# Expert steps of 1,792 hidden units in a one-core diffusion backbone with routed experts

## The chip, the cores and the metric

The kernel runs on 1 core of one Trainium2 chip. The metric is device time in microseconds (us) of one execution; three runs of the kernel before took 1365.89, 1367.7 and 1370.32 us (median 1367.7). The profile is of one more execution, 1364.95 us long.

## The reference, cut to what matters

Two layers over 256 latent tokens of width 1024. Layer 0 is attention and a dense SwiGLU; layer 1 is a pooling mixer and then the part that the change is about, 8 experts of 3,584 hidden units of which each token takes two:

```python
def swiglu(h, w_gu, w_down):
    g, u = jnp.split(h @ w_gu, 2, axis=-1)
    return (jax.nn.silu(g) * u) @ w_down

def moe_swiglu(h, router_w, router_b, w_gu, w_down):
    logits = (h @ router_w).astype(jnp.float32) + router_b.astype(jnp.float32)
    top_v, top_i = lax.top_k(logits, TOP_K)
    gates = jax.nn.softmax(top_v, axis=-1)
    combine = jnp.einsum('btk,btke->bte', gates, jax.nn.one_hot(top_i, N_EXPERTS, dtype=jnp.float32))
    y = jnp.zeros(h.shape, jnp.float32)
    for e in range(N_EXPERTS):
        y = y + combine[..., e:e + 1] * swiglu(h, w_gu[e], w_down[e]).astype(jnp.float32)
    return y.astype(h.dtype)
```

All is float32. The weights of the experts are 8 x 3 x 1024 x 3584 x 4 bytes, 352.3 MB, and each byte is read once.

## The kernel before, in words

The program is written out by hand, engine by engine, with semaphores; nothing schedules it. After the router, the tokens of each expert are gathered into units of 32 slots (`x_all`). In this data the eight experts have 2, 5, 2, 2, 2, 4, 2 and 1 units, 20 in all.

**Steps.** The hidden units of an expert are cut into 4 pieces of 896 (`MS`). A step is one piece of one expert; a round is one step for each of the 8 experts, and there are 4 rounds, so 32 steps. A step has three phases on PE: the gate pass for every unit of the expert, then the up pass for every unit, then the down pass for every unit. The partial results of the 4 rounds are summed in `y_all`.

**Weights and their ring.** A step needs three chunks of 3.67 MB: gate, up, down. They lie in a ring of 5 slots (`RING`, `w_gu`, `w_dn`), chunk c in slot c mod 5. SP issues the loads in the order of use (`load`, `after_step`); ahead of each it waits on the semaphore which says that the chunk five places earlier is used up: a chunk of gate or up is free after the last unit's pass, by halves where the semaphore `pass_half` or `down_half` allows it. A chunk of gate or up comes in 4 DMAs of 896 KB with rows of 896 x 4 = 3,584 bytes (two rows for each partition and DMA); a chunk of down comes in two, with contiguous runs of 16,384 and 12,288 bytes. The first 5 chunks are loaded while the layer before is still at work.

**A pass.** `gate_or_up` runs 8 blocks of the contraction times 4 column tiles of 224 (`W`), in two halves of 4 blocks which go to two PSUM banks. Each half increments `pass_half` or `pass_done`. ACT takes the first half out of PSUM (`take_half`), DVE adds the second (`take_rest`); for gate, ACT then applies SiLU into `kept`; for up, DVE multiplies, transposes and writes the activation back to `kept` (`activate`). POOL brings the tokens (`bring_slots`) and the activations (`bring_act`) of the next unit into place. `down` runs 7 blocks times 4 tiles of 256, again in two halves (4 and 3 blocks), and DVE adds both into `y_all` (`add_rows`). DVE goes in order: it first finishes the `activate` of the last unit, and only then takes the first unit's down result.

**Loops.** PE's program is a loop over 5 steps (the ring's period); inside, each phase is a loop over the units, whose number comes from a register.

**End.** After the last round the rows of `y_all` go to DRAM (`put_rows`), are fetched back by token (`picked`), normalised, and added to the tokens `tok`, which have stayed in SBUF since the mixer.

Of the kernel before, what the change touches and what calls it, by code (L numbers as in the profile page):

```python
# [27 lines left out]
P = 128  # L28
# [21 lines left out]
MS = 896  # L50
MSTEPS = FE // MS
MQ = MS // P
UNIT = 32
# [10 lines left out]
KINDS = 3  # L64
RING = 5
CHUNK = KC * MS * 4
# [67 lines left out]
def build(nc, x, c, ctx_in, c_ctx, ada_w, ada_b, norm_g, w_qkv, w_o, sink, pool_w, pool_b, pool_scale,  # L134
# [10 lines left out]

    w_gu = [sb(f"w_gu{x}", [P, KC, MS], F32, R0 + CHUNK * x) for x in range(RING)]
    w_dn = [sb(f"w_dn{x}", [P, MQ, D], F32, R0 + CHUNK * x) for x in range(RING)]
# [85 lines left out]
    top_i = sb("top_i", [P, 2 * E], U32, S[5] + 4 * KB + 640)  # L233
    y_rows = nc.dram_tensor("y_rows", (SLOTS, D), F32).ap()
# [13 lines left out]
    def col(a, n):  # L248
        return cols[:, a:a + n]
# [14 lines left out]
    R_D, R_EX, R_DEN, R_G1, R_G2 = 48, 50, 52, 54, 56  # L264
# [29 lines left out]
    def bank(i):  # L294
# [14 lines left out]
        halves_free gated_up act_turned act_kept act_lo act_hi down_half down_done y_half y_added late_ident_in places_ready y_written picked0 picked1 f_ready  # L309
# [45 lines left out]
    def _(sp):  # L355
# [36 lines left out]

        GATE, UP, DOWN = range(KINDS)

        def load(x, kind, e, step, parts=range(4)):

            for part in parts:
                if kind == DOWN:
                    if part % 2:
                        continue  # L400
                    rows = slice(2 * part, min(2 * part + 4, MQ))
                    to = w_dn[x][:, rows, :]
                    src = mdn_v[bass.ds(e, 1), bass.ds(step, 1), :, rows, :].rearrange("e s p q n -> p (e s q) n")
                else:
                    rows = slice(2 * part, 2 * part + 2)
                    to = w_gu[x][:, rows, :]
                    src = mgu_v[bass.ds(e, 1), :, rows, bass.ds(step * MS + kind * FE, MS)].rearrange("e p k n -> p (e k) n")
                sp.dma_start(to, src).then_inc(s[f"w_{x}{part // 2}"], 32 if kind == DOWN else 16)  # L408

        load(0, GATE, 0, 0, (0, 1, 2))  # L410
        sp.wait_ge(s["f_split0"], FSTEPS)
        load(0, GATE, 0, 0, (3,))
        sp.wait_ge(s["f_split1"], FSTEPS)
        load(1, UP, 0, 0, (0,))
        sp.wait_ge(s["f_split2"], FSTEPS)
        load(1, UP, 0, 0, (1,))
        sp.wait_ge(s["acc_ready"], (EARLY + L1_LATE) * KC)
        load(3, GATE, 1, 0, (2, 3))
        sp.wait_ge(s["f_used1"], FSTEPS)
        sp.wait_ge(s["f_used2"], FSTEPS)  # L420
        load(2, DOWN, 0, 0, (2,))
        load(3, GATE, 1, 0, (0, 1))
        sp.wait_ge(s["f_used2"], FSTEPS + 1)
        load(1, UP, 0, 0, (2, 3))
        load(2, DOWN, 0, 0, (0,))
        sp.wait_ge(s["poolmix_ready"], TB)
        load(4, UP, 1, 0, (0, 1))
        sp.wait_ge(s["gathered"], 2 * KC)
        load(4, UP, 1, 0, (2, 3))
# [7 lines left out]
        sp.reg_mov(step, 1)  # L437
# [7 lines left out]
        def after_step(t, last=False):  # L445

            next_count(sp, left, n, digit)
            sp.reg_add(gone, gone, n)
            sp.reg_add(passes, passes, n)
            at = place(step)  # L450
            sp.wait_ge(s["pass_done"], passes)
            load(KINDS * t % RING, DOWN, *at)
# [14 lines left out]
        with sp.Fori(0, (STEPS - 2) // RING):  # L467
            for t in range(RING):
                after_step(t)
        assert (STEPS - 2) % RING == 0  # L470
        after_step(STEPS - 2, last=True)
# [24 lines left out]
    def _(pool):  # L496
# [23 lines left out]
        for b in range(TB):  # L520
# [3 lines left out]
        p, d, row, first, at, n, digit = (pool.alloc_register(name) for name in (  # L524
            "pool_pass", "pool_down", "pool_row", "pool_first", "pool_kept", "pool_n", "pool_digit"))
# [4 lines left out]
        pool.reg_mov(d, 1)  # L530

# [10 lines left out]
        def bring_act():  # L542

            a = kept[:, bass.ds(pool.snap(at, min_val=0, max_val=MOST - 1), 1), :].rearrange("p a (q n) -> p (a q) n", n=UNIT)
            pool.wait_ge(s["act_kept"], d)
# [3 lines left out]
            pool.tensor_copy(act_cur[:, 4:MQ, :], a[:, 4:MQ, :]).then_inc(s["act_hi"], 1)  # L549
# [3 lines left out]
        with pool.Fori(0, MSTEPS):  # L553
            pool.reg_mov(first, 0)
            with pool.Fori(0, E):
# [5 lines left out]
                pool.reg_mov(at, 0)  # L561
                with pool.Fori(0, n):
                    bring_act()
# [30 lines left out]
    def _(pe):  # L594
# [408 lines left out]
        def gate_or_up(x, fills):  # L1003

            for half, (bank_, taken, brought) in enumerate(((HALF_BANK, "half_taken", "x_lo"), (REST_BANK, "rest_taken", "x_hi"))):
                pe.wait_ge(s[brought], p)
                pe.wait_ge(s[taken], p)
                pe.wait_ge(s[f"w_{x}{half}"], fills * 32)
                for k in range(4 * half, 4 * half + 4):
                    for t in range(TILES):  # L1010
                        mm = pe.matmul(ps[UNIT * t:UNIT * t + UNIT, bank_, 0:W], x_cur[:, k, :],  # L1011
                                       w_gu[x][:, k, W * t:W * t + W], start=(k % 4 == 0), stop=(k % 4 == 3))
# [805 lines left out]
```

## Time and profile before

| what | value |
|---|---|
| median of 3 runs | 1367.7 us |
| the profiled execution | 1364.95 us, of which the span is 1363.3 us |
| PE busy | 1207.2 us, 89% of the span |
| chain that ended last | PE 67%, DMA 13%, SPq 9%, issue 4%, DVE 4% |
| weights of the experts, issued by SP | 256 DMAs of 896 KB, 32 of 2048 KB, 32 of 1536 KB |
| bytes moved | 461.09 MB, mean 338 GB/s |
| expert stage | from 492.94 us (first pass) to 1337.4 us (last down pass) |

The span is the time from the first to the last instruction on the chip; the execution's own time is 1.65 us more. PE and DMA busy shares near the top at the same time are read stage by stage: the question is which of the two waits for the other.

### The profile page before, as it was taken

What the parts mean: (1) busy time and instruction counts of PE and PEld (TensorE: products, weight loads), DVE (VectorE), ACT (ScalarE), POOL (GpSimd) and SP (SyncE); (2) the same over time, 40 slices, a digit from 0 to 9 for tenths busy, and PEclk for the clock granted to TensorE, in tenths of its full rate; (3) what the DMA queues carried; (4) which work ended last, traced back from release to release, by engine and by line L of the source; (5) the groups of instructions that cost most, each with busy time, mean ns of one, the idle gap of its engine ahead of it and who ended that gap; (6) DMA issues with size and microseconds to landing.
All of it is one profiled execution on the core that took longest, in us unless ns stands there. A gap on an engine that the chain in (4) does not pass through costs nothing.

```text
span 1363.3 us, 43424 instructions
## 1 busy us (share of the span) xinstructions
PE 1207.2 (89%) x16928; PEld 850.5 (62%) x16928; DVE 578.1 (42%) x1110; ACT 316.2 (23%) x535; POOL 169.1 (12%) x518
## 2 busy tenths in 40 slices
PE   4998998999999699998979899968998986999982
PEld 1456975788888576665646466646765643666751
DVE  0588845787775543232222233312332321323322
ACT  2005644334433422111102012111111100211111
POOL 1010000000010111111111111101111110111111
PEclk8899999999999699998989899988998988999995
DMA  9995121688899348899999999999999999999996
GB/s 338 390 366 189 63 93 31 222 293 292 290 337 406 154 174 347 333 410 412 416 409 411 385 408 410 411 414 413 410 410 415 412 410 413 414 385 411 412 416 205
DMA packets 129070, 461.09 MB, mean 338 GB/s; under 512 B 8240, under 2 KB 34016, under 8 KB 120672
## 3 DMA queue, kind: packets, MB, share of 16 engines
q1 hardware_dynamic: 114368, 403.78, 75.4%
q0 software_dynamic: 13952, 55.58, 11.0%
q8 instruction: 68, 1.11, 0.3%
q10 hardware_dynamic: 672, 0.54, 0.1%
q14 instruction: 10, 0.08, 0.0%
HBM read 455.81 MB, written 4.06 MB: 337 GB/s over the span
## 4 chain that ended last, share of the span: by engine, by line
PE 67%; DMA 13%; SPq 9%; issue 4%; DVE 4%; ACT 1%; POOL 0%; POOLq 0%; DVEq 0%; ACTq 0%
PE ps L1011 28%; PE ps L1025 14%; SPq L408 9%; DMA w_gu<-in_moe_w_gu 6%; PE ps L870 4%; PE ps L694 4%; PE ps L822 2%; PE ps L824 2%; PE ps L823 2%; DMA ctx_tok<-in_ctx 2%; PE ps L812 2%; PE ps L754 2%; DMA w_dn<-in_moe_w_down 2%; DMA ada<-in_ada_w 1%; DMA f_raw<-in_ffn_w_gu 1%
## 5 line engine op out<-in xcount | busy, mean ns | idle before, releaser
L1011 PE MATMUL ps<-w_gu,x_cur 128*32 128x224 f32 x10240 | 513.4, 362 | 60.0 <-issue 29.1
L1011 PEld LDWEIGHTS ps<-w_gu,x_cur 128*32 128x32 f32 x10240 | 356.9, 113 | 213.8 <-issue 74.9
L1025 PE MATMUL ps<-w_dn,consts_sb 128*32 128x256 f32 x4480 | 260.4, 386 | 22.3 <-DMA w_dn<-in_moe_w_down 12.2
L1729 DVE TENSOR_TENSOR cols<-cols,ps 128x224 f32<-128x224 f32 x160 | 91.9, 575 | 414.0 <-PE ps L1011 414.0
L1025 PEld LDWEIGHTS ps<-w_dn,consts_sb 128*32 128x32 f32 x4480 | 151.4, 111 | 124.0 <-issue 34.9
L1271 ACT ACTIVATE cols<-ps 128x224 f32<-128x224 f32 x160 | 93.7, 586 | 559.7 <-PE ps L1011 435.7
L1399 DVE SCALAR_TENSOR_TENSOR ada_acc<-ada,cols,ada_acc 128x512 f32<-128x512 f32 x140 | 105.0, 750 | 4.0
L1530 DVE TENSOR_TENSOR f_lo<-f_raw,f_hi 128x2048 fp32r<-128x2048 f32 x32 | 73.1, 2292 | 46.9 <-ACT f_hi L1159 45.6
L536 POOL COPY x_cur<-x_all 128x128 f32 x160 | 47.0, 294 | 317.5 <-PE ps L1011 270.3
L1159 ACT ACTIVATE f_hi<-f_raw 128x2048 fp32r<-128x2048 f32 x32 | 61.0, 1915 | 64.5 <-DMA f_raw<-in_ffn_w_gu 60.5
L822 PE MATMUL ps<-f_hi,hf_hi 128*128 128x512 f32 x176 | 71.1, 404 | 2.9 <-DVE f_act L1571 2.8
L538 POOL COPY x_cur<-x_all 128x128 f32 x160 | 47.0, 293 | 186.6 <-PE ps L1011 186.6
L824 PE MATMUL ps<-f_hi,hf_lo 128*128 128x512 f32 x176 | 69.2, 393 | 0.0
L823 PE MATMUL ps<-f_lo,hf_hi 128*128 128x512 f32 x176 | 69.1, 393 | 0.0
L1286 ACT ACTIVATE kept<-cols 128x224 f32 x80 | 31.2, 390 | 147.8 <-DVE cols L1729 147.8
L1756 DVE TENSOR_TENSOR y_all<-y_all,ps 128x256 f32 x60 | 25.3, 422 | 81.2 <-PE ps L1025 70.0
L1759 DVE TENSOR_TENSOR y_all<-y_all,ps 128x256 f32 x80 | 33.7, 421 | 57.1 <-PE ps L1025 57.1
L547 POOL COPY consts_sb<-kept 128x128 f32 x80 | 23.5, 293 | 175.5 <-DVE kept L1744 106.8
L694 PE MATMUL ps<-wqkv,hT 128*128 128x512 f32 x96 | 42.5, 596 | 1.1 <-DVE hT L1370 1.1
L822 PEld LDWEIGHTS ps<-f_hi,hf_hi 128*128 128x128 f32 x176 | 33.5, 190 | 11.4 <-issue 3.4
L511 POOL DMA_DIRECT2D ada<-in_ada_w x10 | 8.8, 883 | 250.3 <-DVE ada_acc L1399 250.3
L824 PEld LDWEIGHTS ps<-f_hi,hf_lo 128*128 128x128 f32 x176 | 33.3, 189 | 7.2
(236 smaller groups left out, 1074.7 us busy)
## 6 DMA issues: line engine op xcount, KB each, us to landing
w_gu<-in_moe_w_gu SPq DMA_DIRECT2D x256, 896.0 KB
w_dn<-in_moe_w_down SPq DMA_DIRECT2D x32, 2048.0 KB
w_dn<-in_moe_w_down SPq DMA_DIRECT2D x32, 1536.0 KB
ada<-in_ada_w POOLq DMA_DIRECT2D x23, 2048.0 KB, 10.0
f_raw<-in_ffn_w_gu SPq DMA_DIRECT2D x44, 512.0 KB, 6.7
f_raw<-in_ffn_w_down SPq DMA_DIRECT2D x11, 1024.0 KB, 5.0
wqkv<-in_attn_w_qkv SPq DMA_DIRECT2D x3, 2048.0 KB, 19.5
wo_sb<-in_attn_w_o SPq DMA_DIRECT2D x1, 4096.0 KB, 23.7
```

The source lines that it names most:

```text
L408: sp.dma_start(to, src).then_inc(s[f"w_{x}{part // 2}"], 32 if kind == DOWN else 16)
L694: mm = pe.matmul(bank(3 + u % 4), src[:, k, b * P:(b + 1) * P], wqkv[:, k, 512 * n:512 * n + 512], start=(k == 0), stop=(k == KC - 1))
L822: pe.matmul(bank(1 + b), hi, f_hi[k][:, kk, :], start=first, stop=False)
L823: pe.matmul(bank(1 + b), hi, f_lo[k][:, kk, :], start=False, stop=False)
L824: mm = pe.matmul(bank(1 + b), lo, f_hi[k][:, kk, :], start=False, stop=last)
L1011: mm = pe.matmul(ps[UNIT * t:UNIT * t + UNIT, bank_, 0:W], x_cur[:, k, :], w_gu[x][:, k, W * t:W * t + W], start=(k % 4 == 0), stop=(k % 4 ...
L1025: mm = pe.matmul(ps[UNIT * t:UNIT * t + UNIT, bank_, 0:OW], act_cur[:, q, :], w_dn[x][:, q, OW * t:OW * t + OW], start=(q == rows[0]), sto ...
L1159: act.activation(f_hi[k][:], f_raw[k][:], ACT.Copy).then_inc(s[f"f_hi{k}"], 1)
L1271: act.activation(halves.rearrange("p (q c) -> p c q", q=MQ), ps[:, HALF_BANK, 0:W].rearrange("p (c q) -> p c q", q=MQ), ACT.Copy).then_inc ...
L1399: ins = dve.scalar_tensor_tensor(acc_q[:], w[:, k, :], v, acc_q[:], ALU.mult, ALU.add)
L1530: dve.tensor_tensor(lo[:], f_raw[k][:], hi[:].bitcast(F32), ALU.subtract).then_inc(s[f"f_split{k}"], 1)
L1729: dve.tensor_tensor(view, view, ps[:, REST_BANK, 0:W].rearrange("p (c q) -> p c q", q=MQ), ALU.add).then_inc(s["rest_taken"], 1)
```

## The change

A step is now 1,792 units, so there are 2 rounds and 16 steps. A step has six chunks of the same 3.67 MB: gate, low half of the contraction (rows 0 to 511 of the model width) and high half, up low and high, down rows low and high. A pass of a unit reads two chunks, low then high. The loads of gate and up are still 896 KB each, with one row of 1,792 x 4 = 7,168 bytes for each partition. The down phase runs in two parts, over all units each, with one chunk each. The ring still has 5 slots. To make room for the wider `kept`, the tokens are written to DRAM after the mixer (`tok_away`) and read back at the end (`tok_back`); a few small columns move to `cols`.

```diff
-MS = 896
+MS = 1792
+DQ = MQ // 2
+KH = KC // 2
-KINDS = 3
+KINDS = 6
 RING = 5
-CHUNK = KC * MS * 4
+CHUNK = KH * MS * 4
...
-                    rows = slice(2 * part, 2 * part + 2)
-                    to = w_gu[x][:, rows, :]
+                    up, k = divmod(kind, 2)
+                    to = w_gu[x][:, part:part + 1, :]
...
+        load(4, DOWN_LO, 0, 0, (0,))
+        sp.wait_ge(s["y_normed"], 6)
+        sp.dma_start(tok_away, tok[:].rearrange("p b d -> p (b d)")).then_inc(s["tok_kept"], 16)
...
         def after_step(t, last=False):
+            slot = [(KINDS * t + kind) % RING for kind in range(KINDS)]
...
-            sp.wait_ge(s["pass_done"], passes)
-            load(KINDS * t % RING, DOWN, *at)
+            sp.wait_ge(s["pass_half"], passes)
+            load(slot[GATE_LO], DOWN_HI, *at)
             sp.reg_add(step, step, 1)
...
+            sp.wait_ge(s["pass_done"], passes)
+            load(slot[GATE_HI], GATE_LO, *at)
             sp.reg_add(passes, passes, n)
             sp.wait_ge(s["pass_half"], passes)
-            load((KINDS * t + 1) % RING, GATE, *at, parts=(0, 1))
+            load(slot[UP_LO], GATE_HI, *at)
             sp.wait_ge(s["pass_done"], passes)
-            load((KINDS * t + 1) % RING, GATE, *at, parts=(2, 3))
+            load(slot[UP_HI], UP_LO, *at)
+            sp.reg_add(gone, gone, n)
             sp.wait_ge(s["down_half"], gone)
-            load((KINDS * t + 2) % RING, UP, *at, parts=(0, 1))
+            load(slot[DOWN_LO], UP_HI, *at, parts=(0, 1))
             sp.wait_ge(s["down_done"], gone)
-            load((KINDS * t + 2) % RING, UP, *at, parts=(2, 3))
+            load(slot[DOWN_LO], UP_HI, *at, parts=(2, 3))
+            sp.reg_add(gone, gone, n)
+            sp.wait_ge(s["down_half"], gone)
+            load(slot[DOWN_HI], DOWN_LO, *at, parts=(0,))
+            sp.wait_ge(s["down_done"], gone)
+            load(slot[DOWN_HI], DOWN_LO, *at, parts=(2,))
...
+        sp.wait_ge(s["tok_kept"], 16)
+        sp.dma_start(tok_back[:].rearrange("p b d -> p (b d)"), tok_away).then_inc(s["tok_back_in"], 16)
...
-        def gate_or_up(x, fills):
+        def gate_or_up(low, high):
...
-                pe.wait_ge(s[f"w_{x}{half}"], fills * 32)
-                for k in range(4 * half, 4 * half + 4):
+                for k in range(KH):
+                    if k % 2 == 0:
+                        pe.wait_ge(s[f"w_{x}{k // 2}"], fills * 32)
...
+            with pe.Fori(0, n):
+                gate_or_up(chunks[0], chunks[1])
+            with pe.Fori(0, n):
+                gate_or_up(chunks[2], chunks[3])
+            for part in range(2):
+                with pe.Fori(0, n):
+                    down(*chunks[4 + part])
```

Two places show how the instructions stand. The first is SP's queue in the loop over the steps, at the load that waits for the end of the first gate phase; `w_dn_55` and `w_gu_51` are slots 0 and 1 of the ring. Before:

```order
L408 ISA [waits pass_done]
L408 DMA w_dn_55<-in_moe_w_down 128x4096
L408 ISA
L408 DMA w_dn_55<-in_moe_w_down 128x3072
...
L408 ISA [waits pass_half]
L408 DMA w_gu_51<-in_moe_w_gu 128x2x896
...
L408 ISA [waits pass_done]
L408 DMA w_gu_51<-in_moe_w_gu 128x2x896
...
L408 ISA [waits down_half]
L408 DMA w_gu_52<-in_moe_w_gu 128x2x896
```

After (slots 2, 3 and 4 are `w_gu_52` to `w_gu_54`):

```order
L415 ISA [waits pass_half]
L415 DMA w_dn_55<-in_moe_w_down 128x4096
...
L415 ISA [waits pass_done]
L415 DMA w_gu_51<-in_moe_w_gu 128x1792
...
L415 ISA [waits pass_half]
L415 DMA w_gu_52<-in_moe_w_gu 128x1792
...
L415 ISA [waits pass_done]
L415 DMA w_gu_53<-in_moe_w_gu 128x1792
...
L415 ISA [waits down_half]
L415 DMA w_gu_54<-in_moe_w_gu 128x1792
```

One chunk was released by the gate phase, one by the up phase and one by the down phase; now two chunks wait for the end of the gate phase, the next two for the end of the up phase.

The second is PE's queue in the first step. Before, a pass reads one slot and the down pass follows:

```order
L1011 MATMUL ps<-w_gu_50,x_cur 32x224 [waits w_00]
L1011 MATMUL ps<-w_gu_50,x_cur 32x224 x15
L1011 MATMUL ps<-w_gu_50,x_cur 32x224 [waits w_01,rest_taken,x_hi]
...
L1011 MATMUL ps<-w_gu_51,x_cur 32x224 [waits w_10]
...
L1025 MATMUL ps<-w_dn_57,consts_sb 32x256 [waits w_20]
```

After:

```order
L1038 MATMUL ps<-w_gu_50,x_cur 32x448 [waits w_00]
L1038 MATMUL ps<-w_gu_50,x_cur 32x448 x7
...
L1038 MATMUL ps<-w_gu_51,x_cur 32x448 [waits w_10,rest_taken,x_hi]
...
L1038 MATMUL ps<-w_gu_52,x_cur 32x448 [waits w_20]
...
L1038 MATMUL ps<-w_gu_53,x_cur 32x448 [waits w_30,rest_taken,x_hi]
...
L1052 MATMUL ps<-w_dn_59,act_cur 32x256 [waits w_40]
...
L1052 MATMUL ps<-w_dn_55,act_cur 32x256 [waits w_00]
```

A pass has as many matmuls as before, of twice the columns, and alternates between two slots for each unit, so both are held until the last unit is through.

## Rows read from the trace of the kernel before

**Rows 1.** The page: the span

```profile
span 1363.3 us, 43424 instructions
```

**Rows 2.** Windows of the expert stage: engines busy, granted clock, DMA share, GB/s

```profile
490.00:520.00 30.00, 27.66 (x554) 18.89 (x556) 9.55 (x18) 6.46 (x13) 5.35 (x19) 1.00 0.82 317
520.00:545.00 25.00, 25.00 (x524) 17.28 (x512) 10.90 (x24) 5.38 (x11) 4.77 (x16) 1.00 0.83 323
545.00:580.00 35.00, 34.58 (x683) 22.86 (x684) 10.50 (x24) 3.78 (x8) 6.43 (x23) 1.00 0.84 335
...
780.00:830.00 50.00, 49.37 (x996) 32.31 (x988) 17.20 (x40) 8.84 (x17) 9.04 (x33) 1.00 0.97 389
...
880.00:930.00 50.00, 36.94 (x605) 23.57 (x596) 10.67 (x25) 4.84 (x10) 5.48 (x20) 0.86 1.02 412
...
1180.00:1230.00 50.00, 49.59 (x992) 32.21 (x988) 18.02 (x42) 6.46 (x12) 9.20 (x33) 1.00 0.98 395
```

**Rows 3.** Timeline of PE: start, us, line, records (two for each matmul)

```profile
492.94 12.31 PE L1011 MATMUL ps<-w_gu,x_cur 128*32 128x224 f32 x256 [2.12 <-POOL x_cur L536]
...
511.54 30.45 PE L1011 MATMUL ps<-w_gu,x_cur 128*32 128x224 f32 x640
...
545.23 12.29 PE L1025 MATMUL ps<-w_dn,consts_sb 128*32 128x256 f32 x224 [0.21 <-DVE y_all L1754]
557.33 12.29 PE L1011 MATMUL ps<-w_gu,x_cur 128*32 128x224 f32 x256
...
773.47 15.07 PE L1011 MATMUL ps<-w_gu,x_cur 128*32 128x224 f32 x256 [5.86 <-issue]
```

**Rows 4.** Windows with one kind of weights in flight (columns as in rows 2)

```profile
1227.00:1240.00 13.00, 12.79 (x264) 8.48 (x260) 5.13 (x12) 2.51 (x5) 2.44 (x9) 1.00 1.03 405
1242.00:1248.00 6.00, 6.00 (x136) 4.25 (x128) 0.99 (x2) 1.58 (x3) 0.88 (x3) 1.00 1.02 427
1253.00:1266.00 13.00, 11.50 (x228) 7.45 (x220) 4.16 (x11) 1.15 (x2) 2.18 (x8) 1.00 1.03 405
1268.00:1274.00 6.00, 6.00 (x132) 5.01 (x128) 1.13 (x2) 1.93 (x4) 1.18 (x4) 1.00 1.03 430
```

**Rows 5.** Timeline of SP's queue: start and length of the issues

```profile
499.90 1.05 SPq L408 DMA_DIRECT2D w_dn<-in_moe_w_down  x2
504.02 11.95 SPq L408 DMA_DIRECT2D w_gu<-in_moe_w_gu  x8
```

**Rows 6.** The DMA view of 496 to 504 us, in 40 slices

```profile
DMA  9999761000000000000000309903246899599599
```

**Rows 7.** Waits of PE in 492 to 1340 us: total, times, longest

```profile
PE ps L1011 <- issue: 29.1, 5, 5.9
```

**Rows 8.** DVE's groups by form: busy, mean ns, idle before

```profile
L1729 DVE TENSOR_TENSOR cols<-cols,ps 128x224 f32<-128x224 f32 x160 | 91.9, 575 | 414.0 <-PE ps L1011 414.0
...
L1530 DVE TENSOR_TENSOR f_lo<-f_raw,f_hi 128x2048 fp32r<-128x2048 f32 x32 | 73.1, 2292 | 46.9 <-ACT f_hi L1159 45.6
...
L1742 DVE STREAM_TRANSPOSE actT<-cols 128x224 f32<-128x224 f32 x80 | 32.9, 411 | 2.7
L1740 DVE TENSOR_TENSOR cols<-cols,kept 128x224 f32<-128x224 f32 x80 | 32.2, 402 | 11.9 <-DVE cols L1729 0.2
L1756 DVE TENSOR_TENSOR y_all<-y_all,ps 128x256 f32 x60 | 25.3, 422 | 81.2 <-PE ps L1025 70.0 <-DVE kept L1744 11.2
L1744 DVE TENSOR_SCALAR kept<-actT 128x224 f32 x80 | 24.6, 308 | 2.8
```

**Rows 9.** Timeline of the end of the kernel

```profile
1327.77 0.35 SPq L476 DMA_DIRECT2D late_ident<-in_consts  x1
...
1328.25 10.67 SPq L345 DMA_DIRECT2D y_rows<-y_all  x10
...
1334.63 2.79 PE L1025 MATMUL ps<-w_dn,consts_sb 128*32 128x256 f32 x24 [1.17 <-DMA w_dn<-in_moe_w_down]
...
1342.94 1.01 POOL L569 DMA_INDIRECT picked<-y_rows,rows_i  x1 [12.60 <-DMA y_rows<-y_all]
```

More of the change, by code:

```diff
@@ L391, in _ @@
             dense_step(st)
-        GATE, UP, DOWN = range(KINDS)
+        GATE_LO, GATE_HI, UP_LO, UP_HI, DOWN_LO, DOWN_HI = range(KINDS)
         def load(x, kind, e, step, parts=range(4)):
             for part in parts:
-                if kind == DOWN:
+                if kind >= DOWN_LO:
                     if part % 2:
                         continue
-                    rows = slice(2 * part, min(2 * part + 4, MQ))
+                    rows = slice(2 * part, min(2 * part + 4, DQ))
+                    at = DQ * (kind - DOWN_LO)
@@ L402, in load @@
                     to = w_dn[x][:, rows, :]
-                    src = mdn_v[bass.ds(e, 1), bass.ds(step, 1), :, rows, :].rearrange("e s p q n -> p (e s q) n")
+                    src = mdn_v[bass.ds(e, 1), bass.ds(step, 1), :, at + rows.start:at + rows.stop, :].rearrange("e s p q n -> p (e s q) n")
                 else:
-                    rows = slice(2 * part, 2 * part + 2)
-                    to = w_gu[x][:, rows, :]
-                    src = mgu_v[bass.ds(e, 1), :, rows, bass.ds(step * MS + kind * FE, MS)].rearrange("e p k n -> p (e k) n")
@@ L408, in load @@
-                sp.dma_start(to, src).then_inc(s[f"w_{x}{part // 2}"], 32 if kind == DOWN else 16)
-        load(0, GATE, 0, 0, (0, 1, 2))
+                    up, k = divmod(kind, 2)
+                    to = w_gu[x][:, part:part + 1, :]
+                    src = mgu_v[bass.ds(e, 1), :, KH * k + part:KH * k + part + 1, bass.ds(step * MS + up * FE, MS)].rearrange("e p k n -> p (e k) n")
+                sp.dma_start(to, src).then_inc(s[f"w_{x}{part // 2}"], 32 if kind >= DOWN_LO else 16)
+        load(0, GATE_LO, 0, 0, (0, 1, 2))
@@ L436, in _ @@
         sp.reg_mov(passes, 1)
-        sp.reg_mov(step, 1)
+        sp.reg_mov(step, 0)
         def place(t):
@@ L522, in _ @@
             pool.tensor_tensor(xm_lo[:, b, :], xm[:, b, :], xm_hi[:, b, :].bitcast(F32), ALU.subtract).then_inc(s["xm_lo_ready"], 1)
-        p, d, row, first, at, n, digit = (pool.alloc_register(name) for name in (
-            "pool_pass", "pool_down", "pool_row", "pool_first", "pool_kept", "pool_n", "pool_digit"))
+        p, d, unit, row, first, at, n, digit = (pool.alloc_register(name) for name in (
+            "pool_pass", "pool_down", "pool_unit", "pool_row", "pool_first", "pool_kept", "pool_n", "pool_digit"))
         left = unit_counts(pool)
@@ L530, in _ @@
         pool.reg_mov(d, 1)
+        pool.reg_mov(unit, 1)
         def bring_slots():
@@ L1032, in step @@
             next_count(pe, left, n, digit)
-            for kind, work in enumerate((gate_or_up, gate_or_up, down)):
-                chunk = KINDS * t + kind
+            chunks = [((KINDS * t + kind) % RING, fills_before + ((KINDS * t + kind) // RING + 1)) for kind in range(KINDS)]
+            with pe.Fori(0, n):
+                gate_or_up(chunks[0], chunks[1])
+            with pe.Fori(0, n):
+                gate_or_up(chunks[2], chunks[3])
+            for part in range(2):
                 with pe.Fori(0, n):
-                    work(chunk % RING, fills_before + (chunk // RING + 1))
+                    down(*chunks[4 + part])
         with pe.Fori(0, STEPS // RING) as i:
@@ L1040, in _ @@
                 step(t, i * KINDS)
-        for t in range(STEPS // RING * RING, STEPS):
-            step(t)
+        step(STEPS - 1)
         pe.wait_ge(s["late_ident_in"], 16)
-        spread_row(N_G + 3 * KC, (4, 5), 10, late_ident[:])
+        spread_row(N_LAST_GAIN, (4, 5), 10, late_ident[:])
     @block.scalar
@@ L1775, in expert_round @@
                     next_pass()
-                with dve.Fori(0, n):
-                    add_rows(fresh)
+                for part in range(2):
+                    dve.reg_mov(row, first_row)
+                    with dve.Fori(0, n):
+                        add_rows(fresh and part == 0)
+                dve.reg_add(first_row, first_row, n)
         dve.wait_ge(s["gathered"], 2 * KC)
```

109 lines of the change are left out of this document (60 added, 49 removed).

## Prediction

> **What bounds the kernel now.** I read the page first for the span [rows 1], then cut the expert stage into windows [rows 2], because PE and the DMA engines are both near full there and only a cut by time tells which waits. The reader is to see in rows 2 that the DMA share stands at 1.02 whenever the stream is unbroken, at 412 GB/s, while PE is idle for a fifth of some windows: the stage goes at the pace of the weights. Five windows have a lower share. Against 1.02 they lose 5.9 + 4.7 + 6.2 + 2.5 + 2.0 = 21.3 us (30 x (1 - 0.82/1.02), and so on). In these, PE is busy nearly all the time: the ring is full, and SP waits for a slot. So the account of the stage is: bytes left at the first pass, divided by the rate, plus the time in which the stream stands.
>
> The bytes: 5 of 96 chunks are loaded ahead, 91 are left, 60 of gate and up and 31 of down. Windows that hold one kind alone [rows 4] give 405 GB/s for gate and up, 427 and 430 for down: 9.06 and 8.57 us for a chunk of 3.67 MB. 60 x 9.06 + 31 x 8.57 = 809 us. From the first pass at 492.9 [rows 3] to the last landing at 1334.6 [rows 9] it took 841.7. With 21.3 standing, 11.4 are left that lie in no window (part landings, and engines of the 16 that end late); I call this the loss at the edges.
>
> PE's prices come from its timeline [rows 3]: 640 records (10 passes) take 30.3 us to the start of what follows, so 3.03 for a pass; 224 records (4 units of down) take 12.1, 3.03 for a unit. After a longer stop PE starts slowly: the phase at 773.47 took 15.07 us for what takes 12.29 elsewhere.
>
> **The change, part by part.**
>
> *Longer rows.* The bytes are the same; rows of gate and up go from 3,584 to 7,168 bytes. No row shows 7,168, so I bound it: not below the 405 of 3,584-byte rows, not above the 428 of down, whose runs are 14,336 bytes on the mean [rows 4]. Per run and per sixteenth of the stream that is 141.6 and 535 ns; a straight line through both gives 273 ns for 7,168 bytes, 420 GB/s, 8.73 us a chunk. I take this: 60 x 0.33 = **-20 us** on a stream that is the bound. Ends: 0, and -29 at 428.
>
> *The ring.* It keeps 5 chunks, but a step of an expert is now six, and PE holds two of them for a whole phase. PE needs 6 x 3.03 = 18.2 us for each unit of a step, the stream 4 x 8.73 + 2 x 8.57 = 52.1 us a step. So experts with 1 or 2 units leave PE waiting, those with 4 and 5 (73 and 91 us) let the stream run ahead, by 21 and 39 us. Before, these leads were half as long, and 5 chunks are 44 us. I walk it through with 1.5 us from a release to the first bytes (the release at 492.94 + 6.06 = 499.0, the issue at 499.90 [rows 5], and the bytes again at 500.5, slice 23 of the row, after 3 us of standing [rows 6]) and, as a choice, 2.5 us from the mean end of a chunk to its use (its 16 parts don't end together; what this leaves out I keep as edges).
> - Expert 0: the ring is full at 495.9; the next chunk (down high) needs the slot of gate low, which both units read until 502.0. It starts at 503.5. The stream stands 8.9.
> - Expert 1, gate 530.5 to 562: down high of this step waits for the last low half, 558, and starts 559.2: stands 3.7. Then the next gate low; next gate high waits for the low slot of up, free at 588, and the stream stands 12.9. Next up high waits for down low (0.6), next down low for down high at 621 (6.6), the next down high for expert 2's second gate unit (1.8). In all 25.6.
> - Experts 2 to 4: PE needs 37.5 us each, the stream 52; the lead is used up, nothing stands, PE waits from expert 3 on.
> - Expert 5, 4 units: 4.3. Experts 6, 7 and 0 wait for weights again.
> - Second round: expert 1 again 22.3, to which comes the stop of PE at the loop's end just behind it (below), 8.4; expert 5 again 4.3.
>
> Sum 73.8 against 21.3: **+52.5 us**.
>
> *PE's stops at the loop's end.* Five stops of 5.8 us wait for nothing but "issue" [rows 7], one at each return of the loop of 5 steps; with the slow start behind it (2.8) about 8.2. With 16 steps there are two. Where the stream is the bound they cost nothing, before and after; the one that lies behind expert 1 in the second round is in the walk. Bounds: 0 and 12 for it.
>
> *ACT and DVE.* Half as many instructions of twice the size. They hide under passes of 6.06 us (taking both halves, product, transpose and copy come to 1.7 us on DVE for each pass now [rows 8], some 2.7 then). One place doesn't hide: PE's second unit of down waits until DVE has ended the last `activate` and taken the first unit's half. Now that is 0.2 us [rows 3]. The four DVE instructions grow by 224 elements each, at 1.04 ns (the slope between the 256 elements of L1756 and the 2048 of L1530 [rows 8]), and L1729 perhaps by its whole 575 ns: 0.8 to 1.4 together. I take 1.0; it counts only where PE is the bound, and the walk has it. The added wait of DVE behind each row holds up only DVE, which is done 1 us after a unit of 3 us.
>
> *Tokens to DRAM and back.* The store of 1 MB stands in SP's queue between two loads, after the mixer, when the stream is idle; behind it only the load that waits for the gather anyway. Nothing. If it landed late, ACT would start late, by some 3 us at worst. The read back stands between `late_ident` and the ten `y_rows` issues [rows 9]. That queue is what the last fetch waits for, until 1342.94, and 1 MB at 405 to 430 GB/s is **+2.5 us**. Ends 0 and 5.
>
> *Edges.* The last chunk's late landing grows as long as the stream never stops; it will stop more often. Between keeping 11.4 and losing all I take 7.4: **-4 us**, ends 0 and -11.
>
> **Sum:** 1364.95 - 20 + 52.5 + 2.5 - 4 = 1396 against the profiled execution, which lies 2.75 below the median of the runs: **1399 us**. Bounds together: the low ends (428 GB/s, no loss at the edges, no extra PE wait) give about 1377; no gain from the rows 1419, with the full edges 1423.
>
> **The rivals.**
>
> *Faster: the ring still covers the heavy experts.* If the stream ran through expert 1's phases as it does before, standing no more than the present 21.3 us, the longer rows would be left: 1367.7 - 20 + 2.5 = 1350. It decides at the point where the lead fits into the free slots: 39 us of lead, 5 slots of 8.73 = 44. For it: present leads of half that size cost only 2 to 2.5 us in later rounds [rows 2]. Against it: during gate, two slots are held to the end, and the three others are full after 26 us of a phase of 30. I give it 0.08.
>
> *Row length does nothing.* Down's higher rate may come from its 1.5 and 2 MB DMAs rather than from its runs, or the 7,168 bytes may be cut into 3,584. Then gate and up stay at 9.06 and all else holds: 1399 + 20 = 1419. For it: every down DMA in the trace is both longer in its run and larger. Against it: the queue is never empty, so the size of one DMA shouldn't matter. 0.15.
>
> The Trainium skill, page "DMA: Bandwidth & Descriptors", sections "Specifications" and "Bandwidth", speaks for this rival: transfers reach line rate from 512 bytes on, and each packet costs about 3 cycles beside one for every 32 bytes. By that 3,584 bytes lose 3 in 115 cycles and 7,168 lose 3 in 227; as an estimate from the page, gate and up would gain 1.3%, 7 us, and the time would be about 1412. This case's trace disagrees: 405 against 428 GB/s is 5.7%, where that rule would allow 2% between these two lengths.
>
> **How the numbers follow.** Forecast 0.77, the faster rival 0.08, the other 0.15. A measurement of this kernel tells about 0.3% (4 us) from no change; both slower cases lie far above, and only a chain of low ends (lead fits in part, rate at its top) comes near: 0.03 for within 0.3%. Faster 0.09, slower 0.88. The range 1377 to 1423 is the low and the high bounds, and holds the second rival.
>
> **What would show it.** Right: windows of gate and up alone at 418 to 424 GB/s; DMA share well under 1 in the two visits of expert 1, about 20 us each, with SP waiting for PE in its up phase; PE busy without a gap there, idle in experts 3, 4, 7 and 0; two "issue" stops; a gap near 1.2 us once in a step before the second unit of down. Wrong: 405 GB/s with 7,168-byte rows (second rival); a share of 1.0 through expert 1 (first rival); PE's passes longer than 6.1 us at full clock, or waits of PE for ACT, DVE or POOL in each pass, which no term has.

## The result, and the profile after

| | before | after |
|---|---|---|
| median of four runs | 1366.8 us (1364.79 to 1370.32) | 1396.7 us (1393.94 to 1400.45) |
| ratio | 1 | 1.0215, 95% interval 1.0189 to 1.0242 |
| profiled execution | 1364.95 us | 1400.45 us |
| expert stage, first pass to last sum in `y_all` | 492.94 to 1337.96 | 494.83 to 1369.86 |

The change costs 30 us; the forecast was 1399 in a range of 1377 to 1423. The profiled execution of after is the longest of its four, 3.75 us above the median. The page of after (of the queue: packets, MB, share of the 16 engines' time):

```profile
span 1398.7 us, 30632 instructions
...
q1 hardware_dynamic: 81888, 405.88, 72.3%
...
PE 61%; DMA 22%; DVE 6%; SPq 5%; issue 4%; ACT 1%; DVEq 0%; POOL 0%; POOLq 0%; ACTq 0%
```

The page of before has for the same queue:

```profile
q1 hardware_dynamic: 114368, 403.78, 75.4%
```

About the same bytes went in fewer packets, so the longer rows were not cut back into the old length. In the chain that ended last, PE went from 67% to 61% of the span and DMA from 13% to 22%: with a longer time, more of it is waiting for weights. Windows of the expert stage (columns as in [rows 2]):

```profile
494.00:530.00 36.00, 33.91 (x404) 13.91 (x408) 10.14 (x15) 4.99 (x6) 3.89 (x14) 0.95 0.73 297
530.00:565.00 35.00, 35.00 (x415) 13.66 (x408) 6.02 (x9) 7.09 (x9) 4.06 (x14) 1.00 0.94 388
565.00:600.00 35.00, 33.75 (x396) 13.09 (x392) 14.50 (x23) 5.37 (x6) 3.44 (x12) 1.00 0.66 269
600.00:640.00 40.00, 40.00 (x640) 21.33 (x632) 9.50 (x20) 3.06 (x4) 6.25 (x22) 1.00 0.83 330
640.00:700.00 60.00, 54.89 (x716) 23.31 (x708) 17.26 (x30) 6.91 (x8) 6.46 (x24) 0.97 1.01 420
700.00:760.00 60.00, 46.28 (x588) 19.30 (x580) 12.53 (x23) 4.92 (x6) 5.74 (x21) 0.94 1.01 421
...
840.00:900.00 60.00, 49.70 (x604) 19.61 (x596) 13.57 (x22) 7.44 (x9) 5.06 (x18) 0.97 0.99 408
...
983.00:1015.00 32.00, 32.00 (x324) 9.93 (x320) 4.78 (x5) 7.68 (x10) 2.97 (x10) 0.95 0.96 396
1015.00:1045.00 30.00, 28.73 (x336) 9.84 (x332) 13.97 (x22) 3.83 (x4) 3.16 (x11) 1.00 0.60 242
1045.00:1095.00 50.00, 45.71 (x675) 22.50 (x670) 9.49 (x20) 3.50 (x5) 6.55 (x23) 0.93 0.72 286
...
1220.00:1290.00 70.00, 67.61 (x879) 28.68 (x875) 19.94 (x34) 9.01 (x11) 8.13 (x29) 0.99 1.00 415
1290.00:1330.00 40.00, 38.76 (x532) 17.61 (x528) 11.27 (x20) 4.99 (x6) 5.19 (x19) 1.00 0.96 393
1330.00:1366.00 36.00, 23.44 (x220) 7.96 (x216) 4.79 (x8) 3.95 (x5) 1.67 (x6) 0.80 1.01 422
```

Read the last three columns. An unbroken stream now has a share of 1.01 and 420 to 422 GB/s, where [rows 2] had 1.02 and 412. But in the two visits of expert 1 (530 to 640 and 983 to 1095) the share falls from 0.94 and 0.96 to 0.60 to 0.83, while PE is busy but for its own stops (4.3 us at the loop's end, 1.3 ahead of the second unit of down). Against 1.01 these windows lose 10.0 in expert 0, 2.4 + 12.1 + 7.1 = 21.6 in the first visit of expert 1 and 1.6 + 12.2 + 14.4 = 28.2 in the second; the windows around expert 5 (840 to 900 and 1220 to 1330) add 1.2 and 2.7. In all 63.7 us, where [rows 2] gave 21.3. The windows with one kind of weights answer to [rows 4]:

```profile
650.00:680.00 30.00, 28.72 (x404) 13.21 (x396) 7.96 (x14) 4.02 (x5) 3.65 (x13) 1.00 1.01 421
685.00:697.00 12.00, 10.73 (x140) 4.12 (x136) 6.09 (x10) 0.97 (x1) 1.31 (x5) 0.95 1.00 423
...
1157.00:1185.00 28.00, 21.34 (x216) 6.78 (x212) 2.77 (x4) 3.96 (x5) 2.02 (x7) 0.88 1.01 419
```

The first and third hold gate and up alone, the second down. Rows of 7,168 bytes run at 419 to 421 GB/s, rows of 3,584 ran at 405. What PE does and waits for (timeline, then waits in 480 to 1380 us: total, times, longest):

```profile
534.15 60.32 PE L1038 MATMUL ps<-w_gu,x_cur 128*32 128x448 f32 x640
...
598.74 27.40 PE L1052 MATMUL ps<-w_dn,act_cur 128*32 128x256 f32 x504 [1.25 <-DVE y_all L1786]
...
762.84 50.86 PE L1038 MATMUL ps<-w_gu,x_cur 128*32 128x448 f32 x512 [5.88 <-issue]
...
1076.38 27.05 PE L1038 MATMUL ps<-w_gu,x_cur 128*32 128x448 f32 x256 [4.29 <-issue]
```

```profile
PE ps L1038 <- DMA w_gu<-in_moe_w_gu: 59.0, 31, 2.8
PE ps L1038 <- issue: 10.2, 2, 5.9
PE ps L1052 <- DVE y_all L1786: 8.9, 7, 1.3
PE ps L1052 <- DVE y_all L1788: 8.8, 7, 1.3
```

Ten passes take 60.1 us from 534.15 to the down at 594.28, 6.0 for each, so the pass itself is no dearer than before (twice 3.03 in [rows 3]). The five stops on "issue" of [rows 7] are two, the gap before the second unit of down went from 0.2 to 1.3 us, 14 times. SP, which issues the loads, waits for PE's gate and up phases. Its waits in after, then the same in before:

```profile
SPq L415 <- PE ps L1038: 355.0, 54, 25.3
```

```profile
SPq L408 <- PE ps L1011: 104.5, 37, 12.3
```

The longest of these waits is 25.3 us, near the length of a whole phase of expert 1 (30 us): that is the ring held by PE. A wait of SP alone doesn't show that the stream stands, since loads issued earlier may still be running; the share in the windows does.

### The profile page after: what moved, and what is told of

It reads as the page before. It is cut to its first block, busy times and chain, and to the rows that moved or that the text cites. A ratio compares the mean times of both kernels' runs of the same rounds, so it can differ in the third digit from the quotient of the medians.

```text
span 1398.7 us, 30632 instructions
## 1 busy us (share of the span) xinstructions
PE 1212.6 (87%) x11808; PEld 656.0 (47%) x11808; DVE 539.6 (39%) x910; ACT 290.2 (21%) x415; POOL 123.1 (9%) x358
## 3 DMA queue, kind: packets, MB, share of 16 engines
q0 software_dynamic: 13952, 55.58, 10.6%
## 4 chain that ended last, share of the span: by engine, by line
PE 61%; DMA 22%; DVE 6%; SPq 5%; issue 4%; ACT 1%; DVEq 0%; POOL 0%; POOLq 0%; ACTq 0%
PE ps L1038 27%; DMA w_gu<-in_moe_w_gu 14%; PE ps L1052 10%; SPq L415 5%; PE ps L719 4%; PE ps L895 3%; PE ps L847 2%; DMA w_dn<-in_moe_w_down 2%; PE ps L849 2%; PE ps L848 2%; PE ps L837 2%; DMA f_raw<-in_ffn_w_gu 2%; PE ps L779 2%; DMA wqkv<-in_attn_w_qkv 2%; DMA ada<-in_ada_w 1%
## 5 line engine op out<-in xcount | busy, mean ns | idle before, releaser
L1038 PE MATMUL ps<-w_gu,x_cur 128*32 128x448 f32 x5120 | 521.7, 566 | 71.4 <-DMA w_gu<-in_moe_w_gu 59.0
L1038 PEld LDWEIGHTS ps<-w_gu,x_cur 128*32 128x32 f32 x5120 | 168.1, 114 | 417.4 <-issue 341.9
L1052 PE MATMUL ps<-w_dn,act_cur 128*32 128x256 f32 x4480 | 254.6, 386 | 33.7 <-DVE y_all L1786 8.9
L1761 DVE TENSOR_TENSOR cols<-cols,ps 128x448 f32<-128x448 f32 x80 | 76.8, 960 | 475.4 <-PE ps L1038 475.4
L1052 PEld LDWEIGHTS ps<-w_dn,act_cur 128*32 128x32 f32 x4480 | 150.1, 111 | 140.9 <-issue 44.9
L1302 ACT ACTIVATE cols<-ps 128x448 f32<-128x448 f32 x80 | 76.2, 953 | 598.6 <-PE ps L1038 598.6
L1788 DVE TENSOR_TENSOR y_all<-y_all,ps 128x256 f32 x60 | 25.3, 422 | 91.0 <-PE ps L1052 86.6
L1317 ACT ACTIVATE kept<-cols 128x448 f32 x40 | 23.1, 578 | 153.2 <-DVE cols L1761 153.2
L557 POOL COPY x_cur<-x_all 128x128 f32 x80 | 23.7, 296 | 273.9 <-PE ps L1038 241.0
L571 POOL COPY act_cur<-kept 128x128 f32 x80 | 23.7, 296 | 242.3 <-PE ps L1052 122.0
L559 POOL COPY x_cur<-x_all 128x128 f32 x80 | 23.7, 296 | 226.5 <-PE ps L1038 226.5
L848 PEld LDWEIGHTS ps<-f_lo,hf_hi 128*128 128x128 f32 x176 | 33.6, 191 | 6.7 <-issue 0.2
```

Of the source, the lines that this page charges most:

```text
L848: pe.matmul(bank(1 + b), hi, f_lo[k][:, kk, :], start=False, stop=False)
L1052: mm = pe.matmul(ps[UNIT * t:UNIT * t + UNIT, bank_, 0:OW], act_cur[:, q, :], w_dn[x][:, q, OW * t:OW * t + OW], start=(q == rows[0]), sto ...
L1302: act.activation(halves.rearrange("p (q c) -> p c q", q=MQ), ps[:, HALF_BANK, 0:W].rearrange("p (c q) -> p c q", q=MQ), ACT.Copy).then_inc ...
L1761: dve.tensor_tensor(view, view, ps[:, REST_BANK, 0:W].rearrange("p (c q) -> p c q", q=MQ), ALU.add).then_inc(s["rest_taken"], 1)
```

## The experiments

**Theory.** The loss is the time in which the stream stands, because PE holds two of the five ring slots through a whole phase; longer rows win a part of it back. **Rivals:** the rate did not matter or came from elsewhere; the loss comes from PE's own small stalls (issue, DVE); it comes from the tokens' way through DRAM. On the chips of the experiments the kernel before had medians of 1367.9, 1368.4 and 1367.1 us, so the change stands there at about 1397 to 1400.

**The change again (after_again).** No edit.

> The changed kernel once more, unaltered, so that the small steps are set against it in ratios from one chip and not against its first four executions (ratio 1.0215, interval 1.0189 to 1.0242, which is plus or minus 3.7 us). Every theory expects the same, a ratio of 1.0215. Below 1.019 the small gains read so far (4 us for the written-out loop, 6 us for ACT taking a half) would have been too large, above 1.024 too small.

1399.2 us, ratio 1.0232 (1.0201 to 1.0263). Below, "the change" is the pair of ratios, 1.0215 and 1.0232. Gains and losses against it are rounded over both, by ratio and by median.

**Short rows in the changed kernel (rows_short).** The loads in the loop over the steps move the same 896 KB in rows of half the length.

```diff
...
-                    to = w_gu[x][:, part:part + 1, :]
+                    rows, cut, wide = slice(part, part + 1), 0, MS
+                    if short:
+                        rows, cut, wide = slice(part // 2 * 2, part // 2 * 2 + 2), part % 2 * (MS // 2), MS // 2
+                    to = w_gu[x][:, rows, cut:cut + wide]
...
```

> The changed kernel with rows of 3,584 bytes again in the loads of the loop (two half rows for each partition and DMA; number and size of DMAs, steps, ring and passes as in the change). Theory of the prediction (row length sets the rate, the ring sets the standing): windows of gate and up alone fall from 421 to 405 GB/s, time 1396.7 + 20 = 1416 us. Rival (rate comes from the size of a DMA, or from something else in the new order): 420 GB/s stays, 1397 us. Rival (PE is the bound, so the stream's rate hardly counts): under +5 us.

1406.73 us, ratio 1.029 (1.0266 to 1.0313): 7 to 10 us over the change. Its queue and windows:

```profile
q1 hardware_dynamic: 112608, 405.88, 73.4%
```

```profile
565.00:600.00 35.00, 33.75 (x400) 13.23 (x396) 14.12 (x23) 5.36 (x6) 3.42 (x12) 1.00 0.67 265
...
650.00:680.00 30.00, 27.90 (x393) 12.83 (x384) 7.87 (x14) 3.98 (x5) 3.62 (x13) 1.00 1.03 406
...
700.00:760.00 60.00, 46.95 (x600) 19.51 (x592) 12.19 (x22) 4.89 (x6) 5.77 (x21) 0.94 1.02 411
...
1045.00:1095.00 50.00, 45.60 (x700) 23.62 (x692) 12.03 (x25) 3.08 (x4) 6.74 (x24) 0.97 0.78 303
```

With gate and up alone the rate fell from 421 to 406, and for the mix to 411, with DMAs of the same size and number: the row's length sets it. The time came out 9 us under the theory's 1416 and above the rivals' 0 and 5 us. It grew by about half of what a rate of 412 in place of 421 asks (334 MB of the 91 chunks: 811 - 793 = 18 us). The other half is in the share: against 1.02, the windows 494 to 600 and 983 to 1095 stand 45 us here, 53 in the change. A slower stream fills the ring later and stands less, so the two terms are not independent.

**Half of PE's work left out, in both kernels (light_after, light_before).** Of each half pass the second and fourth block of the contraction are left out, of each half of down all but two blocks; all loads stay.

In the changed kernel:

```diff
-                for k in range(KH):
+                for k in range(0, KH, 2):
...
-                    (Y_HALF_BANK, "y_half", "act_lo", range(0, 4)), (Y_REST_BANK, "y_added", "act_hi", range(4, DQ)))):
+                    (Y_HALF_BANK, "y_half", "act_lo", range(0, 2)), (Y_REST_BANK, "y_added", "act_hi", range(4, 6)))):
```

> The changed kernel with half of PE's work left out: of every half pass only blocks 0 and 2 of the contraction, of every down half only two blocks; all loads, waits and releases as in the change, so the output is not the reference's. Theory: PE is then never slower than the stream, the ring never holds it up after expert 0, and the time falls by the standing that the walk has, 70 us, to about 1327 us, DMA share 1.01 through the visits of expert 1. Rival (the time is in handovers between the engines, not in PE's holding of slots): the handovers stay, the time falls by less than 35 us.

> The kernel before with half of PE's work left out in the same way, so the output is not the reference's. Theory: only its 21 us of standing go, 1366.8 - 17 to 21 = 1346 to 1350 us. The difference of the two light kernels is then the row length and the token round trip alone: the one of the change 14 to 20 us faster. Rival (row length does nothing): the one of the change 2 to 4 us slower.

light_after 1334.78 us, ratio 0.9757 (0.9734 to 0.9781); light_before 1345.22 us, 0.9837 (0.9816 to 0.9858). Two windows of the first, then two of the second, the start of the stage and its middle:

```profile
490.00:520.00 30.00, 23.27 (x268) 8.55 (x266) 12.66 (x20) 5.60 (x7) 4.94 (x18) 0.94 0.79 314
...
700.00:900.00 200.00, 116.91 (x1112) 37.64 (x1108) 46.16 (x80) 19.14 (x23) 19.33 (x69) 0.72 1.01 422
```

```profile
490.00:520.00 30.00, 24.29 (x398) 14.43 (x396) 11.78 (x22) 9.85 (x20) 7.05 (x25) 0.94 0.82 317
...
700.00:900.00 200.00, 129.83 (x1844) 71.19 (x1840) 56.81 (x131) 28.82 (x57) 32.23 (x115) 0.80 1.02 413
```

With PE fast enough the stream still stands in the visit of expert 0 (0.79 and 0.82); from 520 to 1280 us every window of 25 to 50 us has a share of 1.01 or more in both kernels. The sign turns: the changed layout is 10.4 us faster. What PE costs by its pace is then 1367.9 - 1345.2 = 23 us in the kernel before and 1397 to 1400 less 1334.8, 62 to 65 us, in the change. These are 40 us more, and 10 less for the stream: 30. In the 40 us are PE's small stops as well (see the last experiment), not the holding of slots alone. The sizes missed: light_after was forecast at 1327, 8 us lower, and the pair at 14 to 20 us apart. The matmuls of gate and up were halved in number, but not in time: they took 336.6 us here and 521.7 in the change, at a mean granted clock of 0.72 in the window above, in which PE was idle for 83 of 200 us, where the change has 0.94 to 1.00: the clock was at the lower of its two levels for part of the time. It did not matter, since the stream was the bound.

**The coarse release in the kernel before (coarse_before).** Nothing but one wait is moved: the slot of gate is refilled only when the up phase is over.

```diff
             sp.reg_add(passes, passes, n)
             at = place(step)
+            sp.reg_add(passes, passes, n)
             sp.wait_ge(s["pass_done"], passes)
             load(KINDS * t % RING, DOWN, *at)
...
             at = place(step)
-            sp.reg_add(passes, passes, n)
             sp.wait_ge(s["pass_half"], passes)
```

> The kernel before with one edit: the slot of a gate chunk is given back only after the up phase, not after the gate phase, so two chunks are held for two phases, as in the change, with rows, steps and passes as before. Theory (the slots that PE holds stop the stream at the heavy experts): the walk with this release gives +13 us (10 to 15), about 1381 us, with new standing in the visits of expert 1 in every round. Rival (release order hardly matters, since the queue is 20 us deep and 4 slots are lead enough): under +4 us.

1379.96 us, ratio 1.0075 (1.0052 to 1.0097), 11.6 us slower. Its windows where [rows 2] has 0.82, 0.83, 0.84, 0.97 and 0.98:

```profile
490.00:520.00 30.00, 27.66 (x484) 18.25 (x487) 10.24 (x19) 6.08 (x12) 4.47 (x16) 0.94 0.48 182
520.00:545.00 25.00, 25.00 (x536) 17.83 (x529) 9.46 (x20) 6.55 (x13) 5.36 (x18) 1.00 0.75 298
545.00:580.00 35.00, 34.57 (x672) 22.32 (x668) 11.63 (x28) 3.45 (x7) 6.13 (x22) 1.00 0.95 372
780.00:830.00 50.00, 47.47 (x932) 31.07 (x936) 13.50 (x30) 8.85 (x17) 8.19 (x29) 0.95 0.88 349
1180.00:1230.00 50.00, 49.79 (x1016) 32.41 (x1012) 17.81 (x40) 8.61 (x17) 9.52 (x33) 1.00 0.96 381
```

Against 1.02 they stand 15.9 + 6.6 + 2.4 + 6.9 + 2.9 = 34.7 us, 13.4 more than before, and the time grew by 11.6. About 2 of the 13.4 lie ahead of the stage, since the first pass is at 495.33 here and at 492.94 before; from there to the last sum the profiles give 856.4 against 845.0 us, 11.4 more. The size is as forecast, the places are not: the first window, mostly expert 0, gained 10.0 (with those 2), the visit of expert 1 behind it lost 1.9, and 4.4 and 0.9 came in the windows at 780 and 1180. A later release is enough to make this kernel slower, with PE's work, rows and loop as they were.

**PE's loop written out, in both kernels (unroll_after, unroll_before).**

```diff
-        with pe.Fori(0, STEPS // RING) as i:
-            for t in range(RING):
-                step(t, i * KINDS)
-        step(STEPS - 1)
+        for t in range(STEPS):
+            step(t)
```

These are the lines of the changed kernel; in the kernel before the same loop goes.

> The changed kernel with PE's loop over the steps written out: no return of the loop, so none of its two stops. Theory: only the stop behind expert 1 in the second round lies on the path, -8 us, 1389 us; the one ahead of expert 5 is hidden or paid back. Rival (PE is the bound throughout): both count with their slow start, -14 to -16 us. Rival (the stream has slack there): 0.

> The kernel before with PE's loop over the steps written out: its five stops of 5.8 us go. Theory: the stream is the bound, so only the stops that came just behind or ahead of expert 1 (the two windows at 97% and 98% DMA share, 4.5 us in all) count: -2 to -5 us, 1363 to 1366 us. Rival (each stop with its slow start is on the path): -40 us.

unroll_after 1393.2 us, ratio 1.0195 (1.0172 to 1.0218), 3 to 6 us under the change, where 8 were forecast. Its interval overlaps with that of the change, so the time alone doesn't show the gain. unroll_before 1365.31 us, 0.9971 (0.9958 to 0.9984), 3 us under the kernel before: the fastest version of the study that does all the work, though only just. Both long stops are gone from the changed kernel, and its window 1045 to 1095 shows where that counts:

```profile
1045.00:1095.00 50.00, 50.00 (x744) 28.93 (x736) 13.69 (x26) 5.05 (x6) 6.72 (x24) 1.00 0.83 337
```

The share went from 0.72 to 0.83, 5.5 us less standing; the profile of after_again has 0.75 in this window, and against that it is 4.0. Writing out stops of 29.1 us in the kernel before gave back 3.

**ACT takes the first half of down (act_takes_y).** ACT copies the first half of each down result out of PSUM, so PE no longer waits for DVE; DVE adds from the copy.

```diff
+                for part in range(2):
+                    with act.Fori(0, n):
+                        act.reg_add(gone, gone, 1)
+                        act.wait_ge(s["y_added"], yd)
+                        act.wait_ge(s["down_half"], gone)
+                        act.activation(y_first[:], ps[:, Y_HALF_BANK, 0:OW], ACT.Copy).then_inc(s["y_half"], 1)
+                        act.reg_add(yd, yd, 1)
...
-            dve.wait_ge(s["down_half"], d_after)
+            dve.wait_ge(s["y_half"], d_after)
...
-                dve.tensor_tensor(part, part, ps[:, Y_HALF_BANK, 0:OW], ALU.add).then_inc(s["y_half"], 1)
+                dve.tensor_tensor(part, part, y_first[:], ALU.add).then_inc(s["y_summed"], 1)
```

> The changed kernel, with ACT instead of DVE taking the first half of a down unit out of PSUM (into a 1 KB buffer, from which DVE adds it), so that PE's second unit no longer waits for the last activate: 14 waits of 1.26 us, 17.7 in all, gone. Theory (PE's time counts only in the visits where it holds up the stream: experts 1, 2, 5 and 6): -4 to -8 us, 1390 to 1394 us. Rival (PE's added stops are what made the change slow): -15 to -18 us, 1380 us.

1391.39 us, ratio 1.017 (1.0149 to 1.019): 6 to 9 us under the change. PE's waits for DVE (17.7 us in the change) are gone, and a part comes back as a wait for POOL:

```profile
PE ps L1053 <- POOL act_cur L572: 13.5, 12, 3.6
```

Two of these twelve waits, 7.1 us, stood in the change too; the other ten, 6.4 us, are what is left of the gap where an expert has two units. At experts 1 and 5 it is gone; the down phase of expert 1, in two pieces at 594.28 and 598.74 in the change, is one here:

```profile
588.78 30.41 PE L1053 MATMUL ps<-w_dn,act_cur 128*32 128x256 f32 x560
```

Of the 11 us that are gone for good, 6 to 9 came off the time; the four gaps at experts 1 and 5, where the prediction had PE as the bound, are 5 of the 11. So the gap was no trifle.

**The tokens read back behind the row stores (tok_late).**

```diff
-        sp.wait_ge(s["tok_kept"], 16)
-        sp.dma_start(tok_back[:].rearrange("p b d -> p (b d)"), tok_away).then_inc(s["tok_back_in"], 16)
-
         for first, after in Y_GROUPS:
...
                 put_rows(sp, first, after, t)
+
+        sp.wait_ge(s["tok_kept"], 16)
+        sp.dma_start(tok_back[:].rearrange("p b d -> p (b d)"), tok_away).then_inc(s["tok_back_in"], 16)
```

> The changed kernel, with the read back of the tokens issued behind the ten row stores instead of ahead of them. Theory: the 3.4 us by which the end after the last down pass grew (28.8 against 25.3 us) are this 1 MB in the queue ahead of the stores, so -3 us, 1394 us, and the fetch by token starts 5 us after the last y_all, as before. Rival (the end grew because the stores of the last group sit behind more of other work): 0.

1398.33 us, ratio 1.0217 (1.0198 to 1.0236). By its time alone this is a miss: no gain over 1.0215, at most 2 us over 1.0232. The profiles tell more. From the end of the last sum in `y_all` to the first `picked` it is 7.8 us here:

```profile
1369.23 0.42 DVE L1791 TENSOR_TENSOR y_all<-y_all,ps 128x256 f32 x1 [1.39 <-PE ps L1052]
```

```profile
1377.43 1.02 POOL L594 DMA_INDIRECT picked<-y_rows,rows_i  x1 [16.01 <-DMA y_rows<-y_all]
```

In the six profiles with the read ahead of the row stores (the change twice, rows_short, light_after, unroll_after, act_takes_y) the same stretch is 8.0 to 9.9 us, 8.9 on the mean; in the six without (the kernel before, its three variants, this one, the next) it is 5.0 to 7.8, 6.7 on the mean. As an estimate from these means the read costs about 2.2 us, less than the interval of one timed pair can show.

**The last three edits together (after_all).** The edits of unroll_after, act_takes_y and tok_late in one kernel.

> The changed kernel with three of the earlier edits together: PE's loop written out, ACT takes the first half of down, the tokens read back behind the row stores. Theory (the stream stands because PE holds two ring slots for a phase, and PE's small stalls only lengthen that): the gains add, 4 + 6 + 0, so the time is 10 us under the change, a ratio of about 1.014, still 19 us above the kernel before, and the ring's standing of the first visit of expert 1 stays above 25 us in 494 to 600. Rival (the small stalls are themselves what the change costs): without them little over the kernel before is left, a ratio of 1.005 or less. A second rival: the two edits gain at the same place (PE in the visits of expert 1 and 5) and do not add, a ratio of 1.017.

1388.55 us, ratio 1.0146 (1.0117 to 1.0176): 8 to 12 us under the change, as the theory's 10; the rival's 1.005 lies outside the interval. The second rival's 1.017 lies inside, so whether the two gains add is not shown. Its windows:

```profile
494.00:530.00 36.00, 33.35 (x367) 13.92 (x369) 10.82 (x15) 7.22 (x10) 3.29 (x12) 0.95 0.65 259
530.00:565.00 35.00, 35.00 (x436) 13.98 (x432) 6.22 (x10) 7.87 (x12) 4.29 (x15) 1.00 0.98 409
565.00:600.00 35.00, 35.00 (x401) 12.74 (x393) 13.70 (x21) 6.13 (x8) 3.43 (x12) 1.00 0.64 256
...
1015.00:1045.00 30.00, 30.00 (x359) 11.44 (x352) 13.56 (x21) 4.19 (x5) 3.13 (x11) 1.00 0.59 242
```

PE is full in the windows of expert 1, and the share there is still 0.64 and 0.59. The first three windows stand 12.8 + 1.0 + 12.8 = 26.6 us against 24.5 in the change; but the first pass is 3.6 us later here (498.42), and most of that time the stream waits for the stage to begin. Moved by as much:

```profile
497.59:603.59 106.00, 104.60 (x1240) 40.80 (x1244) 30.70 (x48) 19.86 (x27) 11.57 (x41) 0.98 0.79 321
```

These 106 us have a share of 0.79 and 321 GB/s, where the change has 0.78 and 318 from 494 to 600: about as much standing as in the change. So without the stops of the loop and the waits for DVE (12.5 us of waits for POOL are left) the stream stands as before in the first visit, and the kernel is 21 us behind the one before.

## Why the prediction was right, point by point

**The account** held: bytes over rate, plus the time in which the stream stands. For the profiled execution of after: 334 MB at 421.5 GB/s is 792; standing 64; from the first pass at 494.8 to the last weights, about 1366.9, it took 872; 16 are left for the edges. How much is standing and how much edge hangs on the column that is read. By GB/s (length x (1 - rate/421.5), and 413 for the kernel before) the same windows of after lose 10.6 + 24.1 + 30.8 + 5.7 = 71 us and those of [rows 2] lose 24, and 9 us are left for the edges in both. Where the stream stands in part, a point of share moves fewer bytes: 286 GB/s at 0.72 would be 397 at 1.00, and 422 at 1.01 is 418. A part of the edges is no loss at all: the last half of the fifth chunk is issued only when the tokens are gathered, and in [rows 6] the engines work on it until 497.4, 4.4 us behind the first pass, while the account counts it as loaded ahead.

**Longer rows, -20.** The straight line through two rows of the trace gave 420 GB/s for rows of 7,168 bytes, measured 419 to 421. Before and after, the whole mix went from 413 to 421.5, 16 us instead of 20. What the term missed is that it is no independent summand: taken out of the changed kernel it is worth 7 to 10 us, because where the ring is full a faster stream only waits sooner. In the light kernels, where little stands, the difference is 10.4 us, or 12.6 with the 2.2 of the tokens' read added: more of the 16, but not all.

**The ring, +52.5.** The walk gave 73.8 us of standing, the windows 63.7 by share and 71 by rate: expert 0 8.9 against 10.0 (10.6 by rate), the first visit of expert 1 25.6 against 21.6 (24.1), the second with the stop behind it 30.7 against 28.2 (30.8), expert 5 8.6 against 3.9 (5.7). One entry of the walk doesn't follow from its own times: from 495.9 to 503.5 are 7.6 us, not 8.9. Less the standing before, the ring cost 42 us by share and 47 by rate. light_after and light_before put the cost of PE's pace, edges and small stops included, at 40 us more than before. The sign, the places and the mechanism held, the size was 5 to 10 too large.

**Edges, -4.** By share these were 16, not 7.4, 4.6 more than before; by rate they were 9 in both kernels. Neither shows the gain of 4 that the term claimed, so its reason (a stream that stops more often ends less late) isn't borne out. That the sum was right to 2.3 us at the median is in part luck: the rows brought 4 us less than forecast and the edges took 4 to 9 more, while the ring cost 5 to 10 less. Against the profiled execution, 1400.45, the forecast of 1396 was 4.5 us short.

**Stops at the loop's end.** Two, as forecast, 5.9 and 4.3 us; the one on the path was put at 8.4, and writing out the loop gave back 3 to 6.

**ACT and DVE.** The gap before the second unit of down was put at 1.2 us, and is 1.3; 14 times; taking most of it away gave back 6 to 9 us. The gate and up passes waited for no engine but at the very first, 2.2 us for POOL; two down phases waited 3.6 and 3.5 us for POOL, 7.1 in all, where two waits with 5.1 stood before.

**Tokens, +2.5.** The read back is estimated at 2.2 us. The store costs nothing that shows: the first pass is at 492.94 to 495.79 in the four profiles without the store (the kernel before and its variants) and at 491.60 to 498.42 in the eight with it, 494.6 on the mean of each.

**The rivals.** The faster one needed a lead that fits into the free slots; the share of 0.60 to 0.83 in the visits of expert 1 rules it out. That row length does nothing fell with 419 to 421 GB/s, with the number of packets, and with rows_short. The Trainium skill, page "DMA: Bandwidth & Descriptors", sections "Specifications" and "Bandwidth", would have allowed 1.3% between the two lengths, as an estimate from the page; the runs show 3.7% (405 against 420 GB/s in windows of gate and up alone), so it understates what a longer row brings here.

Not tried: a ring with more or smaller slots in the changed kernel, and the same wide steps with chunks cut by columns, so that PE would release one slot for each part of a phase. So the runs don't separate what two held slots cost from what phases of twice the length cost with the same ring.

## What to carry to other kernels

When weights stream through a ring and the work for each chunk is uneven, look at how many slots the consumer holds at once and for how long, and not only at the size of the ring: here steps of twice the width, with two slots held through each phase, took SP's waits for gate and up from 104.5 to 355.0 us, and PE's pace cost 40 us more, 8 to 12 of them in small stops, where better rows gave 10. Judge the stream by windows of DMA share at full PE; a share well under its unbroken value with PE full is a held ring, and a faster stream wins back only a part of it. A quick way to split the two is the same kernel with part of PE's work left out: if the order of two versions turns round, the transfer is better and the holding is worse.

## What was not expected

- A rate gained is worth half where the ring is sometimes full: 18 us on the stream, 7 to 10 on the time.
- Stalls of one engine add up only at the places where it is the bound: 29.1 us of stops in the kernel before were worth 3; 17.7 us of waits for DVE in the change 6 to 9, with 6.4 come back as waits for POOL.
- The end, from the last sum to the first fetch, varied between 5.0 and 7.8 us over profiles of kernels without the tokens' read. One pair of profiles would have put 3.5 us on a read that costs about 2.2.
